# Attention one stage deeper: probabilities turned at the head of every second step, two probability buffers, pooling maps one step later

## What is computed

```python
z = rms_norm(x) @ w_in                        # q, k, v, qx, pin and three gates
oa = window_attention(q, k, v, bias, sinks)   # 16 heads, 2 kv groups, chunks of 64, 128 keys
ox = memory_attention(qx, mk, mv)             # 4 heads of 128, 256 memory tokens
op = multiscale_pool(pin, w_map, scale)       # 4 groups: trailing mean over 2/4/8/16, minus the token, then a 128x128 map
merged = g0 * (oa @ w_a) + g1 * (ox @ w_x) + g2 * (op @ w_p)
x = x + rms_norm(merged @ w_out)
```

## Time and profile before

| | |
|---|---|
| median of 3 runs | 784.81 us |
| span of the profiled execution, first to last instruction | 782.9 us |
| what lies around the span | 1.9 us |
| TensorE matmul busy | 774.9 us, 99% |
| VectorE, ScalarE, GpSimd busy | 534.6, 360.5, 56.3 us |
| two steps with one unit of window attention, no map | 14.1 us |
| the same with a map | 15.04 us |
| two steps with one memory unit | 15.3 us |
| two plain steps (48 matmuls) | 10.9 us |

### The profile page before, as it was taken

How to read it: one execution, slowest core, us unless ns; L and a number is a source line. 1 busy time by engine, 2 the same in 40 slices (tenths; PEclk the granted TensorE clock), 3 DMA queues, 4 the chain that set the end, 5 groups by cost and what they waited for, 6 DMA issues and landing times.

```text
span 782.9 us, 11398 instructions
## 1 busy us (share of the span) xinstructions
PE 774.9 (99%) x4462; PEld 673.0 (86%) x4462; DVE 534.6 (68%) x640; ACT 360.5 (46%) x586; POOL 56.3 (7%) x101
## 2 busy tenths in 40 slices
PE   8999999999999999999999999999999999999997
PEld 7888878777877888888888899999999999888885
DVE  6765656676434633534764588888888888999897
ACT  6723445444335213214434564445444445675462
POOL 0010001334000000000001110000011110000002
PEclk9999999999999999999999999999999999999999
DMA  8862312213112333323461013333333335214102
GB/s 294 307 193 59 103 55 93 70 54 100 63 54 63 100 107 108 108 79 137 162 246 64 13 56 108 108 107 107 107 107 107 107 134 214 108 54 163 53 0 108
DMA packets 68069, 85.75 MB, mean 110 GB/s; under 512 B 3504, under 2 KB 57536, under 8 KB 68032
## 3 DMA queue, kind: packets, MB, share of 16 engines
q1 hardware_dynamic: 67568, 84.71, 32.5%
q10 hardware_dynamic: 464, 0.53, 0.2%
HBM read 83.12 MB, written 2.11 MB: 109 GB/s over the span
## 4 chain that ended last, share of the span: by engine, by line
PE 96%; DVE 1%; DMA 1%; ACT 0%; SPq 0%; issue 0%; DVEq 0%; POOLq 0%; POOL 0%; ACTq 0%
PE pair L1654 90%; PE pair L1766 1%; PE pair L1748 1%; PE pair L1780 1%; PE pair L1755 1%; DMA raw<-in_w_mem_kv 1%; PE pair L1785 1%; DVE w_lo L460 0%; PE pair L1661 0%; PE pair L1680 0%; DVE rel_row L1354 0%; DVE memT_lo L1284 0%; DVE wo_lo L460 0%; ACT w_hi L455 0%; ACT wo_hi L455 0%
## 5 line engine op out<-in xcount | busy, mean ns | idle before, releaser
L460 DVE TENSOR_TENSOR w_lo<-raw,w_hi 128x1024 fp32r<-128x1024 f32 x66 | 84.2, 1277 | 88.7 <-ACT w_hi L455 88.7
L1654 PE MATMUL pair<-hT_hi,w_hi 128*128 128x512 f32 x336 | 135.5, 403 | 0.0
L1654 PE MATMUL pair<-hT_hi,w_lo 128*128 128x512 f32 x336 | 131.2, 390 | 0.0
L1654 PE MATMUL pair<-hT_lo,w_hi 128*128 128x512 f32 x336 | 130.9, 390 | 0.0
L455 ACT ACTIVATE w_hi<-raw 128x1024 fp32r<-128x1024 f32 x66 | 69.7, 1055 | 101.1 <-PE pair L1654 91.4
L1654 PE MATMUL pair<-T_hi,op_hi 128*128 128x256 f32 x320 | 90.6, 283 | 0.0
L1654 PE MATMUL pair<-T_lo,op_hi 128*128 128x256 f32 x320 | 90.6, 283 | 0.0
L1654 PE MATMUL pair<-T_hi,op_lo 128*128 128x256 f32 x320 | 90.6, 283 | 0.0
L1654 PEld LDWEIGHTS pair<-hT_hi,w_hi 128*128 128x128 f32 x336 | 63.1, 188 | 14.2 <-issue 1.0
L1654 PEld LDWEIGHTS pair<-hT_lo,w_hi 128*128 128x128 f32 x336 | 63.2, 188 | 13.4 <-issue 1.0
L1654 PEld LDWEIGHTS pair<-hT_hi,w_lo 128*128 128x128 f32 x336 | 63.0, 188 | 13.5
(11 more groups left out here) (223 smaller groups left out, 1656.2 us busy)
## 6 DMA issues: line engine op xcount, KB each, us to landing
raw<-in_w_in SPq DMA_DIRECT2D x42, 512.0 KB, 4.8
raw<-in_w_ffn_up SPq DMA_DIRECT2D x22, 512.0 KB, 4.7
raw<-in_w_ffn_gate SPq DMA_DIRECT2D x22, 512.0 KB, 4.3
W<-in_w_ffn_down SPq DMA_DIRECT2D x8, 1024.0 KB, 5.0
raw<-in_w_branch_a SPq DMA_DIRECT2D x8, 512.0 KB, 4.0
raw<-in_w_out SPq DMA_DIRECT2D x8, 512.0 KB, 4.1
raw<-in_w_ffn_down SPq DMA_DIRECT2D x6, 512.0 KB, 5.0
raw<-in_w_mem_kv SPq DMA_DIRECT2D x4, 512.0 KB, 6.8
```

Source lines behind the costliest of these rows:

```text
L460: eng.tensor_tensor(lo, raw_view(s), hi.bitcast(F32), ALU.subtract).then_inc(weights_split, 1)
L1654: ins = pe.matmul(dst, a, b, start=first and n == 0, stop=last and n == 2, skip_group_check=onto)
```

## The change

Turning the probabilities leaves the middle of a product and goes to the head of the next step, in front of the output and the scores. The output of a unit moves two steps later. So at the head of step 15 + 2u TensorE now turns unit u - 1, makes the output of unit u - 2 and the scores of unit u. Since two units are then under way, the probabilities get two buffers by turns (and the last unit a third). ScalarE and VectorE take their copies at the matching places.

The four maps move from steps 25, 27, 29, 31 to 26, 28, 30, 32. The first four `a` products now stand together ahead of the first two `p`/`x` steps, so that the memory head's output at step 41 comes before its use at step 42; `mixed` gets four buffers. The three-bank rule holds for two steps more.

```diff
-    def merge(jp):
-        a = [[("a", 2 * jp)], [("a", 2 * jp + 1)]]
-        return a + [[("p", j), ("x", j)] for j in (2 * jp, 2 * jp + 1)]
-
-    steps += gates(0) + gates(1)
-    steps += merge(0) + gates(2) + merge(1) + gates(3) + merge(2) + merge(3)
+    def merge_a(jp):
+        return [[("a", 2 * jp)], [("a", 2 * jp + 1)]]
+
+    def merge_px(jp):
+        return [[("p", j), ("x", j)] for j in (2 * jp, 2 * jp + 1)]
+
+    steps += gates(0) + gates(1) + merge_a(0) + merge_a(1) + merge_px(0)
+    steps += gates(2) + merge_px(1) + gates(3)
+    for jp in (2, 3):
+        steps += merge_a(jp) + merge_px(jp)
...
     for g in range(4):
-        steps[first + 3 + 2 * g].append(("map", g))
+        steps[first + 4 + 2 * g].append(("map", g))
...
-    probs = sb("probs", 112.5, [P, 8, P])
+    probs_at = [sb(f"probs{i}", a, [P, 8, P]) for i, a in enumerate((112.5, 92, 104.5))]
...
-    mixed = [sb(f"mixed{i}", 192 + 2 * i, [P, SEQ]) for i in range(2)]
+    mixed = [sb(f"mixed{i}", 192 + 2 * i, [P, SEQ]) for i in range(4)]
...
-            free = 3 if UNIT0 - 2 <= step <= UNIT0 + 2 * UNITS + 1 else 4
+            free = 3 if UNIT0 - 2 <= step <= UNIT0 + 2 * UNITS + 3 else 4
...
+        def probs_of(u):
+
+            return probs_at[2 if u == UNITS - 1 else u % 2]
...
# ScalarE
                 if unit_at(s - 2, 0) is not None:
-                    o_hi(unit_at(s - 2, 0))
+                    probsT_copy(unit_at(s - 2, 0))
+                if unit_at(s - 4, 0) is not None:
+                    o_hi(unit_at(s - 4, 0))
...
-                if unit_at(s, 1) is not None:
-                    probsT_copy(unit_at(s, 1))
...
# VectorE
                 if kind == "a" and b == 0:
-                    if u >= 1:
-                        dve.wait_ge(o_full, u)
+                    if u >= 2:
+                        dve.wait_ge(o_full, u - 1)
...
-                if unit_at(s - 2, 0) is not None:
-                    o_lo(unit_at(s - 2, 0))
+                if unit_at(s - 4, 0) is not None:
+                    o_lo(unit_at(s - 4, 0))
...
# TensorE
-                    if midway and k == ks[5 * len(ks) // 8 - 1]:
-                        midway()
...
                 if unit_at(s - 2, 0) is not None:
-                    unit_out(unit_at(s - 2, 0))
+                    unit_turn(unit_at(s - 2, 0))
+                if unit_at(s - 4, 0) is not None:
+                    unit_out(unit_at(s - 4, 0))
                 if unit_at(s, 0) is not None:
                     unit_scores(unit_at(s, 0))
-                midway = (lambda: unit_turn(unit_at(s, 1))) if unit_at(s, 1) is not None else None
                 for t in steps[s]:
-                    tile(t, s, midway)
-                    midway = None
+                    tile(t, s)
```

More of the change, by code:

```diff
@@ L780, in probsT_copy @@
                 act.wait_ge(probs_turned, u + 1)
-                act.activation(probs[:, :, :], turned[:, :, :].rearrange("p a (b k) -> p (a b) k", b=4), ACT.Copy)\
+                act.activation(probs_of(u)[:, :, :], turned[:, :, :].rearrange("p a (b k) -> p (a b) k", b=4), ACT.Copy)\
                    .then_inc(probsT_ready, 1)
@@ L786, in exps @@
                 kind, a, b = unit_of(u)
+                probs = probs_of(u)
                 act.wait_ge(neg_max_ready, u + 1)
@@ L823, in merged_hi @@
                 act.wait_ge(mixed_ready, j + 1)
-                act.activation(mrg_hi[:, j, :], mixed[j % 2][:, :], ACT.Copy).then_inc(mrg_hi_done, 1)
+                act.activation(mrg_hi[:, j, :], mixed[j % 4][:, :], ACT.Copy).then_inc(mrg_hi_done, 1)
             def mem_hi_of(k):
@@ L1239, in merge @@
                     dve.wait_ge(mixed_ready, j)
-                dst = mixed[j % 2] if kind == "a" else part
+                dst = mixed[j % 4] if kind == "a" else part
                 dve.tensor_tensor(dst[:, :], bk(bank_of[n]), gate, ALU.mult).then_inc(tile_merged, 1)
@@ L1243, in merge @@
                 if kind != "a":
-                    ins = dve.tensor_tensor(mixed[j % 2][:, :], mixed[j % 2][:, :], part[:, :], ALU.add)
+                    ins = dve.tensor_tensor(mixed[j % 4][:, :], mixed[j % 4][:, :], part[:, :], ALU.add)
                     if kind == "p":
@@ L1251, in merged_lo @@
                 dve.wait_ge(mrg_hi_done, j + 1)
-                dve.tensor_tensor(mrg_lo[:, j, :], mixed[j % 2][:, :], mrg_hi[:, j, :].bitcast(F32), ALU.subtract)\
+                dve.tensor_tensor(mrg_lo[:, j, :], mixed[j % 4][:, :], mrg_hi[:, j, :].bitcast(F32), ALU.subtract)\
                    .then_inc(mrg_split, 1)
@@ L1662, in turn_to, with tile @@
                 ins.then_inc(rows_turned, 1)
-            def tile(t, s, midway=None):
+            def tile(t, s):
                 kind, i = t
@@ L1765, in unit_turn @@
                     at = i if u < A_UNITS else 4 * (i % 2) + i // 2
-                    ins = pe.transpose(turned[:, at // 4, P * (at % 4):P * (at % 4) + P], probs[:, i, :], ident[:, :])
+                    ins = pe.transpose(turned[:, at // 4, P * (at % 4):P * (at % 4) + P], probs_of(u)[:, i, :], ident[:, :])
                 ins.then_inc(probs_turned, 1)
```

## The result

The changed kernel takes 787.58 us (median of 6 executions, 786.40 to 788.69) against 784.75 for the kernel before (784.40 to 784.81). The ratio is 1.0036, with a 95% interval of 1.0026 to 1.0046: slower. The six executions form two groups, 786.40, 786.47 and 786.90, and 788.25, 788.33 and 788.69, with nothing in between. The profiled one, 788.33 us, is of the upper group. Four slow executions are in no median here: 851.0, 1006.3 and 1568.3 us of the kernel before, and 1293.7 us of run 5.

The account below looks back on a forecast made before the run. TensorE, busy 99% of the span, was taken to bound the kernel. 784.81 - 0.96 (turning) + 2.53 (new wait) = 786.38, so 786.4 us, with 785.3 to 788.3 to hold 8 in 10.

Parts of the forecast that it names:

- The new wait: Step 27: the gate waits for the bank of step 25's pin product, held through GpSimd's group 1; 2.53 us, once.
- No second wait: After step 27: the copy of step 26's gate still ends before TensorE needs its bank, 0.4 us to spare.
- VectorE's idle time before the copy: Before the copy of the last pin product: VectorE idle for some 9 us, as a sign in the trace.
- GpSimd alone is faster: GpSimd's group 1 after map 0: takes 4.51 us instead of 6.22, as VectorE is idle then.
- The rival of a slow GpSimd: GpSimd's group 1 stays as slow as before: wait 4.24 us, time 788.1 us; chance 0.15.
- The turning: Turning moved out of the product to the step's head: saves 0.96 us in all, unit periods 14.0 instead of 14.1.
- 12 x 0.08 = 0.96 us: Twelve units each save the 0.08 us lost when a product resumes after the turning.
- The lower bound of that term: The turning's gain: nothing, if the output behind a turning lost twice as much as expected.
- The clock: Rival: the wait lowers TensorE's clock, the product behind it runs at half clock, 5.4 us more, 791.8 us; chance 0.03.
- a wait of 2.5 us should leave it: Granted clock stays unchanged by step 27's wait, as it read 1.00 over 4 us after the matmuls at 777.2.
- Its own range: The forecast's total without rivals: 785.4 us (2.0 gained) to 787.2 us (nothing gained, 2.4 us wait).
- Slower: Whole kernel: measurably slower than before, beyond about 0.2% or 1.57 us; chance 0.59 with the rivals.

Follow-up runs that it names:

- run 5: The changed kernel with the scaling and short correction of GpSimd's group 1 left out; 786.01 us, ratio 1.0018.
- run 1: The changed kernel with the four maps back in steps 25, 27, 29 and 31; 784.66 us, ratio 0.9999.
- run 3: The changed kernel with the last pin product copied into a buffer of its own, maps as in the change; 784.14 us, ratio 0.9994.
- run 2: The kernel before with only the four maps moved one step later; 790.70 us, ratio 1.0073.
- run 8: The kernel before with the maps one step later and the last pin product's own buffer; 784.77 us, ratio 1.0002.
- run 11: The changed kernel measured again, nothing altered; 786.94 us, ratio 1.0038.
- run 6: The changed kernel with two more adds in GpSimd's group 1, their result overwritten; 791.31 us, ratio 1.0082.

## Why the prediction was right, and where not

- **The new wait: right, in place, chain and size.** Forecast 2.53 us between the scores and the gate of step 27, measured 2.48. Runs 1 and 3 take it away in two ways, run 2 makes it by the maps alone. "No second wait" was right for the change. A slip beside it: VectorE's idle time before the copy was put at some 9 us, where the prediction's own terms (12.0 + 4.76 - 9.5) give the 7.3 that the trace has.
- **GpSimd alone is faster: right.** Taken 4.51 us for group 1, measured 4.47. The rival of a slow GpSimd (788.1 us) falls, although its time is near the median: the agreement is chance. The rule of the Trainium skill, page "SBUF — State Buffer", section "SBUF: two separate sides", that the two engines take the shared ports by an exclusive lock, is borne out: with VectorE idle both slow rows are gone. In run 1, where VectorE works beside group 1 again, they are back (3.02 us for the two adds, 1.47 for the scaling). That one engine waits until the other's instruction has ended is seen in run 8, where both end within 0.02 us of each other.
- **The turning: direction right, size wrong.** The step "12 x 0.08 = 0.96 us" measured about 0.15 for the turning alone (run 1), and 0.34 with the maps' place, a gain that the sum didn't have. I expected the loss behind a product (0.09) for the output behind a turning, counted from the 0.80 us at which the product came back. It starts at 0.97. By the starts alone that is 0.08 + 0.09 won and 0.17 lost, nothing; the 0.04 us a window unit that are left lie in the product, whose matmuls stand 0.231 us apart behind a return (82.43 to 84.05, seven distances). The lower bound of that term, nothing, was the nearer one, and the periods are 14.09 us instead of the 14.0 forecast.
- **The clock: wrong.** It had a chance of 0.03, at 5.4 us. It fell in 6 of 13 executions, for 1.6 us. The step that failed is "a wait of 2.5 us should leave it", drawn from a stretch at the end of the kernel where the record still said 1.00. The next stretch of that same trace has the fall, 4.9 us after the last matmul:

```profile
782.00:782.90 0.90, 0.00 (x0) 0.00 (x0) 0.00 (x0) 0.00 (x0) 0.00 (x0) 0.54 0.03 9
```

And it was one draw of many. The end of the kernel is the same in all 13 profiles of this case, and from TensorE's last matmul to the fall it takes between 2.8 us (run 11) and 5.2 us (runs 1 and 5). Inside the attention it is 2.8 us from the end of the scores in the changed kernel, 2.6 in run 2 and 2.5 in run 6. By these numbers a wait of 2.5 us stands at the edge. Short matmuls ahead of the idle time are not needed for the fall, since the end of the kernel has none; whether they make it come sooner, and what decides in which execution the clock falls, stays open.
- **The sum.** With the measured terms: 784.75 - 0.34 + 2.48 + 0.11 = 787.0 for the lower group, which lies at 786.4 to 786.9 (some 0.3 less than the terms give, which is not explained), and 788.6 with the 1.58 of the clock, for 788.25 to 788.69. The forecast of 786.4 is at the lower edge of the lower group, with a gain put 0.6 too high and no restart in it. (Its own range should begin at 785.3, not 785.4: 784.81 - 2.0 + 2.53.) The median of six, 787.58, fell between the groups, where no execution is, and that of the seven of run 11 is 786.94. Both lie in the range of 785.3 to 788.3, but with one more execution of the six in the upper group the first would have been at its edge: that much of the hit is luck. "Slower", at 0.59, came true, by the wait that was forecast.

## What to carry to other kernels

Moving a small operation by one step moves everything that waits for it. Here a map of two matmuls, 0.86 us, one step later left a chain over GpSimd and VectorE 3.0 us (2.1 without the turning at the head) instead of 8.5, and the chain takes 5.5; ask of each moved operation which buffer its consumers still hold, and who waits for that. Where the chain can't be shortened, a buffer more can cut it. And on TensorE a wait of a few microseconds may be paid twice, so compare single executions, not only the median: two groups with nothing between them are a hint at the clock. A margin in front of VectorE can be eaten by GpSimd where an instruction of VectorE with two inputs in SBUF meets one of GpSimd's (run 8), so look at where the two meet and not only at the sum of VectorE's own rows.

## What the hardware showed that was not expected

- The granted clock after one wait of TensorE between heads of short matmuls and a product: 1.51 us, full in 9 of 9 executions by their times; 2.48 us, at 0.50 in 6 of 13; 3.35 and 4.7 us, no execution of 4 and 4 as low as the wait alone would give. The fall came 0.3 us after work had begun again in one profile, and inside the wait in two (runs 2 and 6).
- A stretch at 0.50 lasted 3.4 us in the changed kernel's profile and 6.8 us in those of runs 2 and 6, each worked out from the means of the stretches.
- At the end of the kernel, where TensorE has nothing more to do, the fall came 2.8 to 5.2 us after its last matmul, in 13 profiles.
- Ten matmuls or 21 transposes without use in the wait kept it at 1.00: in both profiles, and by their times in 15 of 15 executions.
- An instruction of VectorE on 8 columns with two inputs in SBUF took 0.95 us instead of 0.17, until GpSimd's instruction had ended (run 8).
- Eight transposes cost 0.97 us until an output starts behind them, 0.80 until a product's matmul does, and 1.03 until the scores start, when they stand behind an output.
